# Last units of two modulation pieces on TensorE, x loaded behind four units, warming in doses, two later units moved

## The reference, cut to what matters

```python
c_act = jax.nn.silu(c)
for l in range(DEPTH):                                   # DEPTH = 2
    mod = c_act @ ada_w[l] + ada_b[l]                    # ada_w[l]: 2048 x 6144
    shift, scl, gate_res = jnp.split(mod[:, None, :], 3, axis=-1)
    h = _rms(x, norm_g[l]) * (1.0 + scl) + shift
    z = h @ w_in[l]                                      # even: pool mixer, MoBA; odd: DSA, conv module
    ...
    x = x + gate_res * ((y * jax.nn.silu(g)) @ w_out[l])
```

## Time and profile before

| what | value |
|---|---|
| median of 3 timed runs | 977.73 us |
| lowest, highest | 975.18, 978.46 us |
| profiled execution, its own time | 980.4 us |
| span of the profiled instructions | 978.2 us |
| mean granted TensorE clock | 0.988 of full |

### The profile page before, as it was taken

How to read it: one execution, slowest core, us unless ns; L and a number is a source line. 1 busy time by engine, 2 the same in 40 slices (tenths; PEclk the granted TensorE clock), 3 DMA queues, 4 the chain that set the end, 5 groups by cost and what they waited for, 6 DMA issues and landing times.

```text
span 978.2 us, 18859 instructions
## 1 busy us (share of the span) xinstructions
PE 949.8 (97%) x7098; PEld 915.3 (94%) x7098; DVE 823.2 (84%) x1260; ACT 422.2 (43%) x726; POOL 63.0 (6%) x76
## 2 busy tenths in 40 slices
PE   5999999999999999999999999999999999999998
PEld 5887889999999999999999999999999989998887
DVE  5878979988998879988888899888999986878964
ACT  4110144445565444343444443444555655744331
POOL 1000000010110000222100000000011100000000
PEclk9899999999999999999899999999999999999999
DMA  9999988898876878899858555543445445587962
GB/s 370 412 403 402 413 307 285 317 360 326 306 282 234 300 259 332 313 356 351 303 188 311 186 175 187 178 155 133 170 173 194 172 160 206 197 315 284 366 225 77
DMA packets 76084, 261.27 MB, mean 267 GB/s; under 512 B 7777, under 2 KB 8417, under 8 KB 74097
## 3 DMA queue, kind: packets, MB, share of 16 engines
q1 hardware_dynamic: 73680, 251.38, 69.8%
q0 software_dynamic: 2336, 8.98, 2.5%
HBM read 256.07 MB, written 4.19 MB: 266 GB/s over the span
## 4 chain that ended last, share of the span: by engine, by line
PE 69%; DVE 20%; DMA 6%; issue 2%; ACT 2%; SPq 1%; DVEq 0%; ACTq 0%
PE bank L837 12%; PE bank L839 11%; PE bank L838 11%; PE bank L858 6%; DVE wlo L1206 6%; DMA ada<-ada_units 6%; PE bank L894 5%; DVE acc L1216 5%; PE bank L981 4%; PE bank L983 4%; PE bank L984 4%; PE bank L856 3%; DVE Y L1433 2%; PE bank L928 2%; DVE acc L1236 1%
## 5 line engine op out<-in xcount | busy, mean ns | idle before, releaser
L504 ACT ACTIVATE whi<-raw 128x1024 fp32r<-128x1024 f32 x258 | 272.2, 1060 | 389.0 <-PE bank L839 212.3
L1206 DVE TENSOR_TENSOR wlo<-raw,whi 128x1024 fp32r<-128x1024 f32 x258 | 314.8, 1235 | 74.1 <-ACT whi L504 73.1
L837 PE MATMUL bank<-hhi,whi 128*128 128x256 f32 x912 | 262.5, 288 | 3.2 <-DVE wlo L1206 1.5
L838 PE MATMUL bank<-hlo,whi 128*128 128x256 f32 x912 | 258.0, 283 | 0.0
L839 PE MATMUL bank<-hhi,wlo 128*128 128x256 f32 x912 | 257.9, 283 | 0.0
L1216 DVE SCALAR_TENSOR_TENSOR acc<-ada,cact,acc 128x1024 f32<-128x1024 f32 x140 | 181.4, 1296 | 27.9 <-DMA ada<-ada_units 21.0
L837 PEld LDWEIGHTS bank<-hhi,whi 128*128 128x128 f32 x912 | 174.8, 192 | 6.1 <-issue 3.1
L838 PEld LDWEIGHTS bank<-hlo,whi 128*128 128x128 f32 x912 | 174.9, 192 | 0.1
L839 PEld LDWEIGHTS bank<-hhi,wlo 128*128 128x128 f32 x912 | 174.8, 192 | 0.0
L981 PE MATMUL bank<-whi,hhi 128*128 128x256 f32 x512 | 146.7, 287 | 0.0
L983 PE MATMUL bank<-whi,hlo 128*128 128x256 f32 x512 | 144.8, 283 | 0.0
(11 more groups left out here) (194 smaller groups left out, 1286.9 us busy)
## 6 DMA issues: line engine op xcount, KB each, us to landing
raw<-w_slabs SPq DMA_DIRECT2D x258, 512.0 KB, 4.5
ada<-ada_units SPq DMA_DIRECT2D x152, 512.0 KB, 6.4
pre<-ada_units SPq DMA_DIRECT2D x40, 512.0 KB, 15.4
raw<-w_slabs SPq DMA_DIRECT2D x6, 1024.0 KB, 16.1
V<-w_slabs SPq DMA_DIRECT2D x3, 1024.0 KB, 15.1
Y<-w_slabs SPq DMA_DIRECT2D x3, 1024.0 KB, 14.7
X<-xT SPq DMA_DIRECT2D x2, 1024.0 KB, 6.2
x_dram<-X POOLq DMA_DIRECT2D x4, 512.0 KB, 8.4
```

The lines of the kernel that those rows point to most:

```text
L504: act.activation(whi[:, slot], raw[:, slot], ACT.Copy).then_inc(hi_done, 1)
L837: mm(out, whi[:, s, k, :], ahi[:, c, :], start=(c == 0), stop=False)
L838: mm(out, whi[:, s, k, :], alo[:, c, :], start=False, stop=False)
L1206: dve.tensor_tensor(wlo[:, s], raw[:, s], whi[:, s].bitcast(F32), ALU.subtract)\
```

## The change

Of piece 0 DVE adds units 0 to 13, of piece 1 units 16 to 30. PE multiplies the remaining ones (14 and 15; 31) itself, with the unit as the stationary operand and one column of `cact` as the moving one (`add_unit`, eight matmuls each), into the same PSUM columns, and the reduction then adds to them (`start=p >= 2`). The matmul that reduces column 0 of the piece counts these units as done in `ada_done`. The blocks of 24 and 16 `keep_warm` become doses of four, each behind a unit that DVE has done (three doses for piece 0, two for piece 1). SP issues x behind the first four units. DVE does eleven units ahead of `rsqrt`, not nine. In `UNIT_RATES` slabs 37, 43 and 47 get two units for one, slabs 45, 57 and 61 one for two; SP's steps 48 to 61 and DVE's 52 to 55 and 60 to 61 are written out without a loop.

```diff
--- before.py
+++ after.py
@@ -46,8 +46,8 @@
 PIECES = [("h", 0, 0), ("h", 0, 1), ("h", 0, 2), ("h", 0, 3), ("h", 1, 0), ("h", 1, 1), ("gate", 0, 0),
           ("gate", 0, 1), ("h", 1, 2), ("h", 1, 3), ("gate", 1, 0), ("gate", 1, 1)]
 
-UNIT_RATES = ((10, 34, 2), (34, 45, 1), (45, 47, 2), (47, 48, 1), (48, 62, 2),
-              (62, 70, 1), (70, 72, 2), (110, 111, 2), (112, 113, 2), (115, 117, 1), (121, 125, 1), (125, 132, 2))
+UNIT_RATES = ((10, 34, 2), (34, 37, 1), (37, 38, 2), (38, 43, 1), (43, 44, 2), (44, 46, 1), (46, 57, 2),
+              (57, 58, 1), (58, 61, 2), (61, 62, 1), (62, 70, 1), (70, 72, 2), (110, 111, 2), (112, 113, 2), (115, 117, 1), (121, 125, 1), (125, 132, 2))
 H_PIECE = {0: (0, 1, 2, 3), 1: (4, 5, 8, 9)}
 GATE = {0: 6, 1: 10}
 WIDE = (12, 8)
@@ -325,9 +325,6 @@
                     sp.dma_start(unit_at(n + u), ada_units[bass.ds(unit, 1)].rearrange("a p n -> p (a n)"))\
                       .then_inc(ada_in[unit_slot(n + u)], 16)
 
-            for part in range(2):
-                sp.dma_start(X[:, HC * part:HC * (part + 1), :], xT[:, HC * part:HC * (part + 1), :])\
-                  .then_inc(x_in[part], 16)
             def load_halves(p, first, last):
                 for n in range(first, last):
                     unit, half, u = UNITS * p + n, n // 8, n % 8
@@ -337,7 +334,11 @@
                                            PIECE // 2 * half:PIECE // 2 * (half + 1)]
                                  .rearrange("a p n -> p a n")).then_inc(ada_in[unit_slot(unit)], 16)
 
-            load_units(0, UNITS, None)
+            load_units(0, 4, None)
+            for part in range(2):
+                sp.dma_start(X[:, HC * part:HC * (part + 1), :], xT[:, HC * part:HC * (part + 1), :])\
+                  .then_inc(x_in[part], 16)
+            load_units(4, UNITS - 4, None)
             load_wide(sp, 0)
             load_units(UNITS, 3, None)
             load_wide(sp, 1)
@@ -359,7 +360,7 @@
             for w0, w1 in ((10, 14), (14, 22), (22, 34), (34, 48), (48, 62), (62, 72),
                            (72, 91), (91, 99), (99, 110), (110, 125), (125, 131),
                            (131, 132), (132, N_SLABS - AHEAD)):
-                if w0 in (10, 34, 62, 110, 131):
+                if w0 in (10, 34, 48, 62, 110, 131):
                     for w in range(w0, w1):
                         step(w, None)
                 else:
@@ -925,7 +926,8 @@
                         pe.wait_ge(mod_done, p)
                     if p >= 6:
                         pe.wait_ge(o_copied, HC if p < 10 else 2 * HC)
-                ins = mm(sums(p, j)[:, j:j + 1], acc[:, p % 2, j * P:(j + 1) * P], ones[:, 0:1], start=True, stop=True)
+                ins = mm(sums(p, j)[:, j:j + 1], acc[:, p % 2, j * P:(j + 1) * P], ones[:, 0:1],
+                         start=p >= 2, stop=True, skip_group_check=p < 2)
                 if j == HC - 1:
                     ins.then_inc(mod_sum, 1)
                 return ins
@@ -1049,16 +1051,34 @@
             for i in range(KC):
                 x_stat(i)
             spread_token(0)
-            keep_warm(24, O[:, SEQ:SEQ + P])
+
+            def warm_until(units, last):
+                for u in range(units, last + 1):
+                    pe.wait_ge(ada_done, u + 4)
+                    keep_warm(4, O[:, SEQ:SEQ + P])
+
+            def add_unit(p, k, first):
+                unit = UNITS * p + k
+                pe.wait_ge(ada_in[unit_slot(unit)], 16 * unit_uses(unit, None))
+                for j in range(HC):
+                    mm(sums(p, j)[:, j:j + 1], unit_at(unit)[:, j * P:(j + 1) * P], cact[:, k:k + 1],
+                       start=first and j % (HC // 2) == 0, stop=False, skip_group_check=True)
+
+            added = (14, 15)
 
             halved = (2, 3)
 
             def reduce_half(p, half):
-                pe.wait_ge(ada_done, UNITS * p + 8 * (half + 1) + 4 if p in halved else UNITS * (p + 1) + 4)
-                if not half and p:
+                if p in halved:
+                    pe.wait_ge(ada_done, UNITS * p + 8 * (half + 1) + 4)
+                elif not half:
+                    pe.wait_ge(ada_done, UNITS * p + added[p] + 4)
+                if not half and p in halved:
                     pe.wait_ge(mod_done, p)
                 for j in range(4 * half, 4 * half + 4):
                     ins = reduce_part(p, j, half=True)
+                    if p not in halved and j == 0:
+                        ins.then_inc(ada_done, UNITS - added[p])
                 if not half:
                     ins.then_inc(half_sum, 1)
 
@@ -1066,7 +1086,12 @@
                 p = c // GROUP
                 if c % GROUP == 0 and p not in halved:
                     if p:
-                        keep_warm(16, O[:, SEQ:SEQ + P])
+                        warm_until(UNITS + 13, UNITS + 14)
+                        pe.wait_ge(mod_done, p)
+                    else:
+                        warm_until(11, 13)
+                    for k in range(added[p], UNITS):
+                        add_unit(p, k, k == added[p])
                     reduce_half(p, 0)
                     reduce_half(p, 1)
                 if c % GROUP == GROUP - 1 and p + 1 in halved:
@@ -1461,16 +1486,16 @@
                 norm_x(0, GROUP * p + 3)
 
             dve.wait_ge(acc_zero, 1)
-            add_units(0, 9, None)
+            add_units(0, 11, None)
             dve.wait_ge(stat_done, KC)
             rsqrt(0, QT, M[:, 0:QT], D_MODEL)
             token_diag()
-            add_units(9, 7, None)
+            add_units(11, 3, None)
             dve.wait_ge(r_copied, 1)
             first_half(0)
             second_half(0)
             dve.wait_ge(acc_zero, 2)
-            add_units(UNITS, 16, None)
+            add_units(UNITS, 15, None)
             dve.wait_ge(acc_zero, 3)
             first_half(1)
             second_half(1)
@@ -1573,7 +1598,8 @@
             step_o(O0, 0)(51, None)
             keep_piece(7)
             dve.wait_ge(xr_in[1], 16)
-            run(dve, 52, 56, step_o(O0, 0))
+            for w in range(52, 56):
+                step_o(O0, 0)(w, None)
             dve.wait_ge(mod_done, GATE[0] + 2)
             dve.wait_ge(xr_in[2], 16)
             step_o(O0, 0)(56, None)
@@ -1581,7 +1607,8 @@
             step_o(O0, 0)(58, None)
             step_o(O0, 0)(59, None)
             dve.wait_ge(xr_in[3], 16)
-            run(dve, 60, 62, step_o(O0, 0))
+            step_o(O0, 0)(60, None)
+            step_o(O0, 0)(61, None)
             step_o(O0, 0)(62, None)
             lo(65, None, (0,))
             for g in range(2):
```

## The result

Over 19 runs each the changed kernel takes 981.27 us (median, 979.20 to 986.75), the kernel before 977.21 (975.09 to 980.83). The ratio is 1.0044, 95% interval 1.0033 to 1.0056: 4.3 us slower by the ratio (the medians lie 4.1 apart), more than the 0.3% that counts as a change here.

The account below looks back on a forecast made before the run. PE was busy 97% of the span, and unit 48's landing was taken to bound the start. 980.4 (profiled execution) + 4.5 - 3.0 + 0.2 = 982.1, less 2.7 to the median: 979.4 us, range 974.0 to 984.0.

Parts of the forecast that it names:

- +4.5: Start of the kernel: the change makes it 4.5 us slower, bounds 0 and +8.0.
- set by bytes alone: Start: unit 48 lands at 96.49, fixed by the bytes issued ahead, so DVE cannot begin it sooner.
- the sum: Start: PE's 3.3 us delay less about 1.3 of DVE idle time before unit 48, plus 2.5 for the clock.
- The 40 one-column records: Piece 0 on PE: added units and half a reduction, 4.6 us at full clock, 8.1 at half, taken 6.5.
- a sign of being wrong: Start: a granted clock of 1.00 through the units added on PE would show the forecast wrong.
- The clock ahead of chunk 4: Start, before chunk 4: the clock falls after one-column work and idle time, costing 0 to 3.4 us, taken 2.5.
- The first rival: Start free because PE multiplies at full clock, output projection still gains: 974.9 us, chance 0.22.
- deciding point of 67.4: Start: chunk 4 time from which unit 48 is late; the first rival expected chunk 4 at 65.5.
- the projection's -3.0: First output projection, slabs 57 to 61: units sooner and a stall shortened gain 3.0 us, bounds -3.8 and 0.
- The 1.7 of clock: First output projection: half of a 3.4 us stretch at clock 0.50 after PE's 2.11 idle, expected to be regained.
- The units moved forward: Slabs 37, 43, 47: extra units cost +0.2 us, bounds 0 and 1.4; slab 47's last gated chunk about a microsecond later.
- The second rival: Start costs 4.5 us, output projection gains nothing since PE's 2.11 stall stays: 982.4 us, chance 0.22.

Follow-up runs that it names:

- start_only: The change without its new UNIT_RATES and without the loops written out, against the kernel before: 981.88 us, ratio 1.0044.
- x_late: The kernel before with x behind four units and eleven units ahead of the reciprocal root, nothing else: 977.17 us, ratio 1.0013.
- p0_only: The change, but in piece 1 DVE adds all sixteen units and PE runs 16 keep-warm matmuls: 980.59 us, ratio 1.0046 to the kernel before.
- p1_only: The change, but in piece 0 DVE adds all sixteen units and PE runs 24 keep-warm matmuls: 979.20 us, ratio 1.0030 to the kernel before.
- p1_kw16: The kernel before with unit 31 multiplied by PE behind the full block of 16 keep-warm matmuls: 979.75 us, ratio 1.0024.
- moves_only: The kernel before with the later units moved and the loops written out, its start untouched: 976.24 us, ratio 0.9996.

## Why the prediction was right, and where it was off

**The direction of the start was right, and its size.** +4.5 was said; 4.2 is in the trace of the change and 4.3 in the runs of `start_only`. Unit 48's landing bounds the kernel before: chunk 4 at 65.02, 65.11, 65.96 and 66.10 all give unit 48 within 0.07 us of 96.57. But the landing is not set by bytes alone, as the prediction had it. With x first and the unit in its old place it falls at 96.31 to 96.54 in six kernels; with x behind four units, and the same bytes ahead, at 96.82 to 98.17 in the other six, which go with 354 to 408 GB/s from 4 to 10 us, where with x first it is 414 to 420. Why the queue is slower there isn't shown. In `x_late` and `p0_only` this later landing is what DVE waits for. Where it isn't, the sum runs as it was made: the delay of chunk 4, plus the clock's part of DVE's wait, less 1.26. For the change 3.28 + 1.69 - 1.26 = 3.7, and unit 48 is 3.84 late; for `p1_only` 1.42 + 2.95 - 1.26 = 3.1, and 3.2 are there. In the eight kernels where DVE doesn't wait for the landing, unit 48 is 0.1 to 0.5 later than this sum.

**Its terms were off in both directions.** x landed 5.89 later, not 5.1, so `x_stat` ended at 26.75, not 25.9: the prediction had taken 410 GB/s where the queue carried 364. The 40 one-column records took what they take at full clock, which the prediction had named as a sign of being wrong: 3.63 for 32, and the bias addition came 4.64 behind their beginning, where 6.5 was taken, at 37.99 and not 39.0. But the lower clock then fell almost wholly into the chunks: four took 23.8, not 22.8. So chunk 4 came at 69.38 for a forecast 69.4 because errors cancelled, which is luck. The clock ahead of chunk 4 cost 1.69, where 2.5 was taken.

**The first rival** had the records right (full clock) and its conclusion wrong: the sum came at 37.99, not 37.1, and chunk 4 at 69.38, over its own deciding point of 67.4. One-column work ran at full clock behind warming, and the clock fell right behind it (0.50 from 38.73, chunk 0 from 39.46).

**The step that failed is the projection's -3.0.** Its stall was sized well. PE's wait for DVE from 425 to 470 is 2.1, 2.0, 1.5, 0, 0.9 and 1.8 us in the six kernels with the old slabs 48 to 63, mean 1.4, and 0.9, 0, 0, 0, 0, 0.4, 0.8 and 0 in the eight with the new ones, mean 0.3: a gain of 1.1 for a forecast 1.3. Two things were wrong around it.

The 1.7 of clock was taken as the kernel's. A stretch at 0.50 near 461 is in two of the six (before, `p1_kw16`) and in none of the eight; by that count it is worth 0.6, not 1.7. It belongs to some executions only, and that of the kernel before was a long one: from slab 48 to 78 the kernel before took 193.2 us in its profile, the five others with the same code there 186.8 to 189.95. The prediction scaled its sum down by 2.7 because that execution was long, and then also took off a clock that had helped to make it longer.

The units moved forward were given 0.2. Slabs 45 to 50 take 1.09 longer, the last gated product 1.07 later, as the prediction's sentence on slab 47 said, though it took only 0.2 for it; 0.7 comes back in slabs 51 to 56 (35.1 in five of six kernels with two units in 47, 35.8 to 35.9 in four of six without). With 0.4 the sum is -1.1 - 0.6 + 0.4 = -1.3, inside the interval of `moves_only`, -1.8 to +1.0 us, which doesn't tell it from zero. In the change even that didn't show: the whole lost what its start alone lost, so the forecast's net rise of 1.7 was 4.3. The second rival (the start costs, the projection gains nothing, 982.4) is thus the nearest in time, at 1.1 us, though not by its mechanism: the stall did go.

**Not separated:** how the 4.3 us divide between x behind four units and the units on PE. x first saves 1.8 (1.0044 to 1.0026), x late alone costs 1.3 with an interval to zero, unit 31 alone costs 2.3, and piece 0's part with x late costs 4.5 without unit 31; the parts meet in one slack of 1.26 and one falling clock and don't add up.

## What to carry to other kernels

Work moved from a vector engine to TensorE was paid twice here where it was one-column work ahead of dense matmuls: in its own time, and in the clock of what followed; so look at the granted clock behind such work, not only in it. Find first what bounds the stretch (here the landing of one unit): an engine freed ahead of it gains nothing, and a delay beyond the slack is lost whole. Check too whether the change moves that landing itself, as a new order of loads did here. And when a sum is shifted from a profiled execution to the median, a stall or a low-clock stretch that may be that execution's own must not be counted again; the same code in other kernels' traces shows whether it is.

## What the runs showed of the hardware

One-column fp32 matmuls took 0.113 us per record behind warming and 0.213 without (32 records, 3.63 and 6.83). In the change PE ran 3.7 us of them without idle time ahead of chunk 4, then idled 0.69, and the granted clock was 0.50 from 69.45. In the kernel before 1.84 us of them and the same 0.69 stood there, and the clock stayed at 1.00. The Trainium skill ("TensorE: Matmul & The Clock Gate", Part 1) says that the clock follows how busy the engine has lately been; the busy time of the profile does not tell these two apart.

Where the stretches at 0.50 fall differs between executions of the same instructions. Ahead of chunk 0 it lay at 34.43 to 41.26 in the kernel before and at 36.27 to 39.68 in `moves_only`, whose start is the same, and chunk 4 came 1.1 us apart. That may be part of why runs of one kernel spread over some 6 us; the runs without a trace don't show it.
